# The start of a 12-stage network on one core: x loaded first, its squares summed along rows, scale before shift

## The chip, the cores and the metric

The kernel runs on one core of one Trainium2 chip. The metric is the device time of one execution in microseconds (us). Five engines work side by side, each with its own queue of instructions: TensorE (PE, matrix products), VectorE (DVE), ScalarE (ACT), GpSimd (POOL) and SyncE (SP, which here only starts transfers). They wait for each other through semaphores. An engine's transfers are carried by DMA queues: SP's go through q1, ACT's through q10, POOL's through q0, all on the same 16 DMA engines.

## The reference, cut to what matters

The network has twelve stages (a gated linear recurrence, sparse attention, differential attention, a state-space layer and feed-forward layers). The change lies wholly in what comes before the first matrix product of the first of them:

```python
c_act = jax.nn.silu(c)
mods = jnp.einsum('bd,lde->lbe', c_act, ada_w) + ada_b[:, None, :]
shift, scale, gate = jnp.split(mods[0], 3, axis=-1)

def rms_norm(x, gain):
    y = x32 * lax.rsqrt(jnp.mean(x32 * x32, axis=-1, keepdims=True) + EPS)
    return (y * gain).astype(x.dtype)

h = rms_norm(x, norm_mix[0]) * (1 + scale[:, None, :]) + shift[:, None, :]
q, f, i, g = jnp.split(h @ w_in, ...)          # the first matrix product
```

x is 512 tokens by 1024 features. c has 1024 entries, and the layer's shift and scale are 2 x 1024 numbers from a 1024 x 2048 piece of ada_w. All data are float32.

## The kernel before, in words

Features lie on the partitions: xT holds x as 8 tiles (kt = 0 to 7) of 128 features by 512 tokens. x arrives as rows (xin, 4 tiles of 128 tokens by 1024) and TensorE turns it, four 128x128 transposes a tile, into banks 0 to 3 of PSUM. ScalarE makes the square of each turned tile (sq, two buffers) and copies the tile to xT (lines 2160, 2161). TensorE multiplies sq by a matrix of ones, so that bank 7 holds the sum of squares of each token, on all partitions (line 535). ScalarE makes rstd = 1/sqrt(mean + eps) of it (2177, 2178).

The modulation: c and the biases come in as rows (vec_a), TensorE turns them, VectorE copies them to cols_a, and ScalarE makes cact = silu(c), 8 columns of 128. The 1024 x 2048 piece of ada_w arrives in 8 slices of 128 rows (ada_first, 1 MB each, 6 buffers; slices 6 and 7 wait on SP until slices 0 and 1 were used). Columns 0 to 1535 of each slice are taken by VectorE, which multiplies them by cact and adds them up in ada_sum (lines 524, 527); at the end TensorE sums ada_sum over the partitions with 12 products of one column (line 556). Columns 1536 to 2047 are taken by TensorE directly, 4 products of one column a slice (line 544). Each such product is two passes (float32) in the trace. All 16 results are columns of PSUM bank 4: 0 to 7 are shift, 8 to 15 are scale. VectorE adds the bias (mods, 2381), makes gain = (1 + scale) x norm_mix (gains_a, 2373), and signals mods_rdy.

A weight product is done in three parts for accuracy: weights as whi + wlo, activations as hh + hl. ScalarE rounds raw to whi (line 385), VectorE makes wlo = raw - whi (line 389). Then `apply` runs over the eight tiles: VectorE xn = xT x gain x rstd (2402), ScalarE hh = rounded xn + shift (2185), VectorE hl = xn + shift - hh (2394). TensorE's first block of products waits for wlo and takes each tile as hh and hl come (lines 426, 430); later blocks are line 448. raw has two buffers, and the load of the third block waits for wlo of the first.

The order on each engine is the order in which the code is written. On TensorE it is: turn vec_a; slices 0 and 1; x with its ones products; slices 2 to 7, with the transpose of vec_b (the norm gains, for cols_b) after slice 3; the 12 sums. The x load stands sixth in ScalarE's queue of issues, behind the constants; `ones` is the last of these, and TensorE's first instruction waits for all of them (const_a).

Of the kernel before, what the change touches and what calls it, by code (L numbers as in the profile page):

```python
# [17 lines left out]
ACT = mybir.ActivationFunctionType  # L18
# [51 lines left out]
def build(nc, a, out, upto=99):  # L70
    ctx = ExitStack()
    with ctx:
# [162 lines left out]
        const_a, const_in = sem("const_a_in"), sem("const_in")  # L235
        x_in = sem("x_in")
        sq_rdy, ssq_rdy, rstd_rdy = sem("sq_rdy"), sem("ssq_rdy"), sem("rstd_rdy")
# [280 lines left out]
        def ada_first_dve(dve, link):  # L518

            for kt in range(FIRST):  # L520
                dve.wait_ge(ada0_in[kt % 6], 16 * (kt // 6 + 1))
                w, c = ada_first[:, kt % 6, 0:NV * P], cact[:, kt:kt + 1]
                if kt == 0:
                    nc.vector.tensor_scalar(ada_sum[:, :], w, c, None, ALU.mult).then_inc(ada0_sum_v, 1)
                else:
                    dve.wait_ge(ada0_sum_v, kt)
                    nc.vector.scalar_tensor_tensor(out=ada_sum[:, :], in0=w, scalar=c, in1=ada_sum[:, :],
                                                   op0=ALU.mult, op1=ALU.add).then_inc(ada0_sum_v, 1)
            dve.wait_ge(cols_ps, 2)
            link(nc.vector.tensor_copy(cols_b[:, 0:NROW_B], ps[:, 5, 0:NROW_B]))  # L530

        def first_square_sum(pe, kt):

            pe.wait_ge(sq_rdy, kt + 1)
            nc.tensor.matmul(ps[:, 7, :], ones[:, :], sq[:, kt % 2, :], start=(kt == 0),
                             stop=(kt == KT - 1)).then_inc(ssq_rdy, 1)

        def ada_first_pe(pe, k0, k1):
# [15 lines left out]
            pe.wait_ge(ada0_sum_v, FIRST)  # L554
            for j in range(NV):
                m = nc.tensor.matmul(ps[:, 4, j:j + 1], ada_sum[:, j * P:j * P + P], ones[:, 0:1],
                                     start=False, stop=True, skip_group_check=True)
            m.then_inc(ada0_used, 1)

# [1494 lines left out]
        def _(sp):  # L2054

            for kt in range(FIRST):
                if kt >= 6:
                    sp.wait_ge(ada0_sum_v, kt - 5)
                    sp.wait_ge(ada0_used, kt - 5)
                sp.dma_start(ada_first[:, kt % 6, :], a["ada_w"][0, kt * P:(kt + 1) * P, 0:SLOT]  # L2060
                             ).then_inc(ada0_in[kt % 6], 16)
# [76 lines left out]
        def _(act):  # L2138
# [12 lines left out]
            act.dma_start(ones[:, :], a["k_ones"]).then_inc(const_a, 16)  # L2151
            act.dma_start(xin[:, :, :], a["x"][0].rearrange("(t p) d -> p t d", p=P)).then_inc(x_in, 16)
            act.wait_ge(cols_rdy, 1)
            nc.scalar.activation(cact[:, :], cols_a[:, ROWS["c"]:ROWS["c"] + 8], ACT.Silu).then_inc(cact_rdy, 1)
            log_table()
            for kt in range(KT):
                act.wait_ge(mm, kt + 1)
                if kt >= 2:
                    act.wait_ge(ssq_rdy, kt - 1)
                nc.scalar.activation(sq[:, kt % 2, :], ps[:, kt % 4, :], ACT.Square).then_inc(sq_rdy, 1)  # L2160
                nc.scalar.activation(xT[:, kt, :], ps[:, kt % 4, :], ACT.Copy).then_inc(ev_v, 1)
            act.wait_ge(pool_set, 2)

# [195 lines left out]
        def _(dve):  # L2359
# [20 lines left out]
            dve.wait_ge(cols_rdy, 1)  # L2380
            link(nc.vector.tensor_tensor(mods[:, 0:16], ps[:, 4, 0:16], cols_a[:, 0:16], ALU.add))
            modulated_gain(0, ROWS["norm_mix"], 8).then_inc(mods_rdy, 1)
            if upto >= 2:
                convert_lo(dve, segs[0], 0, 0, 0)

            def apply(j, m, gain, shift, h_free):
# [11 lines left out]
                for kt in range(KT):  # L2398
                    k = KT * j + kt
                    if k >= 2:  # L2400
                        dve.wait_ge(hl_rdy, k - 1)
                    nc.vector.scalar_tensor_tensor(out=xn[:, k % 2, :], in0=xT[:, kt, :],
                                                   scalar=gain[:, kt:kt + 1], in1=rstd[:, :],
                                                   op0=ALU.mult, op1=ALU.mult).then_inc(xn_rdy, 1)
                    if kt:
                        low(k - 1)
# [46 lines left out]
            if upto >= 2:  # L2453
                dve.wait_ge(mods_rdy, 1)
                apply(0, 0, *mod_cols(0), FIRST_UNITS)
# [124 lines left out]
        def _(pe):  # L2580
            pe.wait_ge(const_a, 16 * 5)
            nc.tensor.transpose(ps[:, 6, 0:NROW_A], vec_a[0:NROW_A, :], ident[0:NROW_A, 0:NROW_A]).then_inc(cols_ps, 1)
            ada_first_pe(pe, 0, 2)
            pe.wait_ge(x_in, 16)
            for kt in range(KT):
                if kt >= 4:
                    pe.wait_ge(ev_v, kt - 3)
                for t in range(TT):
                    m = nc.tensor.transpose(ps[:, kt % 4, t * P:(t + 1) * P], xin[:, t, kt * P:(kt + 1) * P],
                                            ident[:, :])  # L2590
                m.then_inc(mm, 1)
                if kt:
                    first_square_sum(pe, kt - 1)
            first_square_sum(pe, KT - 1)

# [55 lines left out]
            if upto >= 2:  # L2651
                ada_first_pe(pe, 2, FIRST)
                linear(seg["h_q"], need=(hl_rdy, 0))
# [131 lines left out]
```

## Time and profile before

| | |
|---|---|
| median of three runs | 3031.37 us (3028.98 to 3031.47) |
| the profiled execution | 3029.0 us, its span 3027.3 us |
| mean granted TensorE clock | 0.968 |
| busy share of the span | PE 93%, DVE 55%, ACT 35%, POOL 2% |
| start of the first weight product | 57.00 us |
| DMA | 321 MB, mean 106 GB/s; about 400 GB/s until 34 us, then none until 55 us |

Times in the views are us from the start of the span. Of a group "x16" the duration is from the first start to the last end. A float32 product shows as two passes, a transpose as one. The granted clock is given as a share of 2.4 GHz, so 0.50 is 1.2 GHz. PEld rows are weight loads, which overlap the products.

### The profile page before, as it was taken

The numbers are of one execution on the slowest core, as the hardware profiler recorded it, in microseconds if no ns is written. First come the engines' busy times: TensorE is split into PE (matmuls) and PEld (weight loads), VectorE is DVE, ScalarE is ACT, GpSimd is POOL, SyncE is SP. The second block draws the span as 40 slices with busy tenths as digits, with TensorE's granted clock in tenths as the row PEclk, the third lists the DMA queues.
The fourth block names the chain that finished last, engine by engine and source line by source line (L and its number), as shares of the span: only waits on it lengthen the run. The fifth ranks groups of instructions, "written<-read, shape, count | busy, mean of one in ns | idle before, by whom it ended". The sixth has DMA issues, their size and how long they took to land.

```text
span 3027.3 us, 38551 instructions
## 1 busy us (share of the span) xinstructions
PE 2827.0 (93%) x14850; PEld 2262.7 (75%) x14850; DVE 1654.6 (55%) x2383; ACT 1063.9 (35%) x1577; POOL 75.2 (2%) x87
## 2 busy tenths in 40 slices
PE   6999999999988799999999998999999977999999
PEld 4898778888776556688787785777887756778787
DVE  4576566766453667433334557467677395353342
ACT  3312233222322367332223438433232534342231
POOL 2013000000000000000000100000000000000000
PEclk9999999999999799999999999999999988999999
DMA  5640356564424000232333330143444671223332
GB/s 212 195 140 1 112 153 191 163 182 144 154 86 128 1 1 1 56 83 81 107 84 111 114 100 13 42 100 103 141 153 153 230 125 57 84 83 98 97 97 70
DMA packets 400811, 321.14 MB, mean 106 GB/s; under 512 B 14409, under 2 KB 387233, under 8 KB 399649
## 3 DMA queue, kind: packets, MB, share of 16 engines
q1 hardware_dynamic: 324096, 237.19, 26.7%
q10 hardware_dynamic: 74496, 77.77, 7.9%
q0 software_dynamic: 2080, 4.26, 0.6%
q8 instruction: 96, 1.57, 0.2%
q14 instruction: 43, 0.34, 0.0%
HBM read 293.05 MB, written 19.86 MB: 103 GB/s over the span
## 4 chain that ended last, share of the span: by engine, by line
PE 64%; issue 22%; DVE 8%; ACT 2%; DMA 2%; POOL 1%; SPq 0%; ACTq 0%; DVEq 0%; POOLq 0%
PE ps L448 45%; PE ps L426 4%; PE ps L442 2%; PE ps L430 2%; DVE ada_acc L1749 1%; PE ps L873 1%; PE ps L903 1%; PE ps L885 1%; PE ps L1617 1%; PE ps L2605 1%; DVE h_area L1751 1%; DVE h_area L1753 1%; DMA xin<-in_x 1%; PE ps L1658 1%; POOL kT L1829 1%
## 5 line engine op out<-in xcount | busy, mean ns | idle before, releaser
L448 PE MATMUL ps<-hh,whi 128*128 128x512 f32 x1744 | 690.8, 396 | 5.1 <-DVE xT L2439 1.6
L448 PE MATMUL ps<-hh,wlo 128*128 128x512 f32 x1744 | 680.7, 390 | 0.0
L448 PE MATMUL ps<-hl,whi 128*128 128x512 f32 x1744 | 680.1, 390 | 0.0
L389 DVE TENSOR_TENSOR wlo<-raw,whi 128x2048 fp32r<-128x2048 f32 x198 | 453.9, 2292 | 359.7 <-ACT whi L385 359.7
L385 ACT ACTIVATE whi<-raw 128x2048 fp32r<-128x2048 f32 x198 | 377.3, 1906 | 380.8 <-PE ps L448 257.7
L448 PEld LDWEIGHTS ps<-hh,whi 128*128 128x128 f32 x1744 | 328.1, 188 | 79.3 <-issue 11.8
L448 PEld LDWEIGHTS ps<-hl,whi 128*128 128x128 f32 x1744 | 328.2, 188 | 70.3 <-issue 3.8
L448 PEld LDWEIGHTS ps<-hh,wlo 128*128 128x128 f32 x1744 | 327.9, 188 | 69.2
L448 PE MATMUL ps<-hid_h,whi 128*128 128x512 f32 x756 | 307.4, 407 | 0.0
L448 PE MATMUL ps<-hid_l,whi 128*128 128x512 f32 x756 | 298.9, 395 | 0.0
L448 PE MATMUL ps<-hid_h,wlo 128*128 128x512 f32 x756 | 298.8, 395 | 0.0
L448 PEld LDWEIGHTS ps<-hid_h,whi 128*128 128x128 f32 x756 | 142.2, 188 | 37.5 <-issue 4.3
L448 PEld LDWEIGHTS ps<-hid_l,whi 128*128 128x128 f32 x756 | 142.2, 188 | 37.4 <-issue 4.3
L448 PEld LDWEIGHTS ps<-hid_h,wlo 128*128 128x128 f32 x756 | 142.0, 188 | 34.6
L510 DVE SCALAR_TENSOR_TENSOR ada_ring<-ada_ring,cact 128x256 f32<-128x256 f32 (+1 forms) x336 | 151.8, 452 | 12.1
L2202 ACT ACTIVATE sq<-xT 128x512 f32 (+1 forms) x56 | 35.3, 632 | 291.5 <-DVE xT L2439 138.8
L2437 DVE TENSOR_TENSOR xT<-xT,ps 128x512 f32 (+1 forms) x40 | 27.4, 686 | 165.8 <-PE ps L448 144.7
L2263 ACT ACTIVATE hid_h<-hid_f 128x512 f32 (+1 forms) x44 | 27.8, 632 | 246.6 <-DVE hid_f L2485 246.6
L426 PE MATMUL ps<-hh,whi 128*128 128x512 f32 x176 | 78.0, 443 | 38.4 <-ACT hh L2185 38.4
L2325 ACT ACTIVATE act_t<-ps 128x512 f32<-128x512 f32 x64 | 38.0, 597 | 194.8 <-PE ps L448 185.9
L2539 DVE TENSOR_TENSOR hid_f<-act_t 128x512 f32<-128x512 f32 x64 | 43.4, 688 | 103.7 <-ACT act_t L2325 103.3
L2485 DVE TENSOR_TENSOR hid_f<-act_t,ps 128x512 f32<-128x512 f32 x44 | 30.2, 687 | 126.3 <-PE ps L448 121.3
(401 smaller groups left out, 4130.8 us busy)
## 6 DMA issues: line engine op xcount, KB each, us to landing
raw<-in_ffn_w_in SPq DMA_DIRECT2D x44, 1024.0 KB, 6.0
ada_ring<-in_ada_w ACTq DMA_DIRECT2D x82, 512.0 KB, 4.4
raw<-in_ffn_w_up SPq DMA_DIRECT2D x32, 1024.0 KB, 5.4
raw<-in_ffn_w_down SPq DMA_DIRECT2D x32, 1024.0 KB, 5.8
raw<-in_ffn_w_out SPq DMA_DIRECT2D x32, 704.0 KB, 4.6
raw<-in_hgrn_w_in SPq DMA_DIRECT2D x16, 1024.0 KB, 5.8
raw<-in_attn_w_qkv SPq DMA_DIRECT2D x12, 1024.0 KB, 5.1
s_area<-cp_dram SPq DMA_DIRECT2D x6, 2048.0 KB, 9.8
```

Source lines behind the costliest of these rows:

```text
L385: nc.scalar.activation(whi[:, par, :], raw[:, par, :], ACT.Copy).then_inc(w_hi, 1)
L389: nc.vector.tensor_tensor(wlo[:, par, :], raw[:, par, :], whi[:, par, :].bitcast(F32), ALU.subtract).then_inc(w_lo, 1)
L426: nc.tensor.matmul(ps[:, 2 * par + j, :], tile(w, kt, j), hi[:, kt, :], start=(kt == 0 and n == 0), stop=False)
L430: m = nc.tensor.matmul(ps[:, 2 * par + j, :], tile(wh, kt, j), lo[:, kt, :], start=False, stop=(kt == k - 1))
L442: m = nc.tensor.matmul(ps[:, bank, half * 256:half * 256 + 256], x[:, kt, t0:t0 + P], w[:, kt, :], start=(kt == 0 and n == 0), stop=(kt == ...
L448: m = nc.tensor.matmul(ps[:, bank, :], tile(w, kt, j), x[:, kt, :], start=(kt == 0 and n == 0), stop=(kt == k - 1 and n == 2))
L510: nc.vector.scalar_tensor_tensor(out=acc if last else w[:, 0, :], in0=w[:, kt, :], scalar=cact[:, kt:kt + 1], in1=w[:, 0, :], op0=ALU.mult ...
L873: m = nc.tensor.matmul(ps[:, S_BANK[w % 2] + i, 0:n], nqr[rows, p, t * P:(t + 1) * P], (k_sel, k_win)[br][rows, p // 2, 0:n], start=False, ...
L885: m = nc.tensor.transpose(ps[:, 2 + i, kt * P:(kt + 1) * P], pbuf[:, 2 * (w % P_SLOTS) + i, kt * P:(kt + 1) * P], ident[:, :])
L2202: nc.scalar.activation(sq[:, q:q + 1, :], xT[:, bass.ds(b * s.dve + j, 1), :], ACT.Square).then_inc(sq_rdy, 1)
L2325: nc.scalar.activation(act_t[:, j, :], ps[:, 2 * par + j, :], ACT.Relu).then_inc(ev_a, 1)
L2539: nc.vector.tensor_tensor(hid_f[:, j, :], act_t[:, j, :], act_t[:, j, :], ALU.mult).then_inc(hidf_rdy, 1)
```

## The change

Four things are changed. x is loaded by SP ahead of all modulation weights, instead of by ScalarE behind the constants. The squares are no longer made from the turned tiles: ScalarE squares each 128-token row tile of xin whole (128x1024) with a running sum along the row, which gives four columns x_ssq of one sum a token. VectorE spreads each column onto the diagonal of a 128x128 tile (ident times the column, in the space of rstd, line 540 of the new kernel), and TensorE multiplies the four by ones (line 547), which puts the sums into bank 7 in the old layout. TensorE's order becomes: x first, with slice 0 after tile 3 and slice 1 after tile 7, then slices 2 and 3, the four ones products, and slices 4 to 7. And of the 12 final sums those of scale come first (four of them, bank 4) with their own signal, then the eight of shift into bank 6; VectorE makes scale, gain and the first two xn before it waits for shift.

```diff
+        def first_square_spread(dve):
+            for t in range(TT):
+                dve.wait_ge(x_sq, t + 1)
+                nc.vector.tensor_scalar(rstd[:, t * P:(t + 1) * P], ident[:, :], x_ssq[:, t:t + 1], None, ALU.mult
+                                        ).then_inc(sq_rdy, 2)
+        def first_square_sums(pe):
+            for t in range(TT):
+                pe.wait_ge(sq_rdy, 2 * t + 2)
+                nc.tensor.matmul(ps[:, 7, t * P:(t + 1) * P], ones[:, :], rstd[:, t * P:(t + 1) * P], start=True, stop=True,
+                                 skip_group_check=True).then_inc(ssq_rdy, 2)
...
-            for j in range(NV):
-                m = nc.tensor.matmul(ps[:, 4, j:j + 1], ada_sum[:, j * P:j * P + P], ones[:, 0:1],
-                                     start=False, stop=True, skip_group_check=True)
-            m.then_inc(ada0_used, 1)
+            for bank, part in ((4, range(KT, NV)), (6, range(KT))):
+                for j in part:
+                    m = nc.tensor.matmul(ps[:, bank, j:j + 1], ada_sum[:, j * P:j * P + P], ones[:, 0:1],
+                                         start=(j == 0), stop=True, skip_group_check=True)
+                m.then_inc(ada0_used, 1)
...
+            sp.dma_start(xin[:, :, :], a["x"][0].rearrange("(t p) d -> p t d", p=P)).then_inc(x_in, 16)
             for kt in range(FIRST):
...
-            act.dma_start(xin[:, :, :], a["x"][0].rearrange("(t p) d -> p t d", p=P)).then_inc(x_in, 16)
...
+            act.wait_ge(x_in, 16)
             for kt in range(KT):
                 act.wait_ge(mm, kt + 1)
-                if kt >= 2:
-                    act.wait_ge(ssq_rdy, kt - 1)
-                nc.scalar.activation(sq[:, kt % 2, :], ps[:, kt % 4, :], ACT.Square).then_inc(sq_rdy, 1)
                 nc.scalar.activation(xT[:, kt, :], ps[:, kt % 4, :], ACT.Copy).then_inc(ev_v, 1)
+                if kt % 2:
+                    t = kt // 2
+                    if t >= 2:
+                        act.wait_ge(x_sq, t - 1)
+                    nc.scalar.activation((sq, xn)[t % 2][:, :, :].rearrange("p s n -> p (s n)"), xin[:, t, :], ACT.Square,
+                                         accum_out=x_ssq[:, t:t + 1]).then_inc(x_sq, 1)
...
-            link(nc.vector.tensor_tensor(mods[:, 0:16], ps[:, 4, 0:16], cols_a[:, 0:16], ALU.add))
-            modulated_gain(0, ROWS["norm_mix"], 8).then_inc(mods_rdy, 1)
-            if upto >= 2:
+            link(nc.vector.tensor_tensor(mods[:, 8:16], ps[:, 4, 8:16], cols_a[:, 8:16], ALU.add))
+            link(modulated_gain(0, ROWS["norm_mix"], 8))
+            def first_shift():
+                dve.wait_ge(ada0_used, FIRST + 2)
+                nc.vector.tensor_tensor(mods[:, 0:8], ps[:, 6, 0:8], cols_a[:, 0:8], ALU.add).then_inc(mods_rdy, 1)
                 convert_lo(dve, segs[0], 0, 0, 0)
...
+                    if j == 0 and kt == 1:
+                        first_shift()
...
-            ada_first_pe(pe, 0, 2)
             pe.wait_ge(x_in, 16)
             for kt in range(KT):
...
-                if kt:
-                    first_square_sum(pe, kt - 1)
-            first_square_sum(pe, KT - 1)
+                if kt % 4 == 3:
+                    ada_first_pe(pe, kt // 4, kt // 4 + 1)
+            ada_first_pe(pe, 2, 4)
+            first_square_sums(pe)
...
-                ada_first_pe(pe, 2, FIRST)
+                ada_first_pe(pe, 4, FIRST)
```

TensorE at the start of the program, in the kernel before. `ada_first` with `cact` are the column products of a slice, `xin` the transposes, `sq` the squares' products; the semaphore waited for stands in brackets.

```order
1 L2582 MATMUL ps<-ident,vec_a 128x120 [waits const_a_in]
2 L544 MATMUL ps<-cact,ada_first 128x1 [waits ada0_in0,cact_rdy]
3 L544 MATMUL ps<-cact,ada_first 128x1 x3
4 L544 MATMUL ps<-cact,ada_first 128x1 [waits ada0_in1]
5 L544 MATMUL ps<-cact,ada_first 128x1 x3
6 L2589 MATMUL ps<-ident,xin 128x128 [waits x_in]
7 L2589 MATMUL ps<-ident,xin 128x128 x7
8 L535 MATMUL ps<-sq,ones 128x512 [waits sq_rdy]
9 L2589 MATMUL ps<-ident,xin 128x128 x4
10 L535 MATMUL ps<-sq,ones 128x512 [waits sq_rdy]
```

The same place in the changed kernel, down to the second slice (between the rows shown, four more groups of four transposes follow slice 0, each waiting for ev_v, a copy by ScalarE):

```order
1 L2603 MATMUL ps<-ident,vec_a 128x120 [waits const_a_in]
2 L2609 MATMUL ps<-ident,xin 128x128 [waits x_in]
3 L2609 MATMUL ps<-ident,xin 128x128 x15
4 L556 MATMUL ps<-cact,ada_first 128x1 [waits ada0_in0,cact_rdy]
5 L556 MATMUL ps<-cact,ada_first 128x1 x3
6 L2609 MATMUL ps<-ident,xin 128x128 [waits ev_v]
7 L2609 MATMUL ps<-ident,xin 128x128 x3
```

Sixteen transposes now stand ahead of slice 0, and slice 1 has moved behind all 32; after the transposes TensorE has this:

```order
14 L556 MATMUL ps<-cact,ada_first 128x1 [waits ada0_in1,cact_rdy]
16 L556 MATMUL ps<-cact,ada_first 128x1 [waits ada0_in2,cact_rdy]
18 L556 MATMUL ps<-cact,ada_first 128x1 [waits ada0_in3]
20 L562 MATMUL ps<-ident,vec_b 128x120 [waits const_in]
21 L547 MATMUL ps<-rstd,ones 128x128 [waits sq_rdy] x4
22 L556 MATMUL ps<-cact,ada_first 128x1 [waits ada0_in4,cact_rdy]
24 L556 MATMUL ps<-cact,ada_first 128x1 [waits ada0_in5]
```

The eight 512-wide products of the squares have become four 128-wide ones between slices 3 and 4. (Of each slice the first product is shown; three more follow it.)

VectorE around the modulation, in the kernel before:

```order
9 L527 SCALAR_TENSOR_TENSOR ada_sum<-ada_first,cact,ada_sum 128x1536 [waits ada0_sum_v,ada0_in1]
10 L530 COPY cols_b<-ps 128x120 [waits cols_ps]
11 L2381 TENSOR_TENSOR mods<-ps,cols_a 128x16 [waits cols_rdy,ada0_used,v_link]
12 L2373 SCALAR_TENSOR_TENSOR gains_a<-mods,cols_b 128x8 [waits v_link]
13 L389 TENSOR_TENSOR wlo<-raw,whi 128x2048 [waits w_hi]
14 L2402 SCALAR_TENSOR_TENSOR xn<-xT,gains_a,rstd 128x512 [waits mm,rstd_rdy,mods_rdy]
15 L2402 SCALAR_TENSOR_TENSOR xn<-xT,gains_a,rstd 128x512
16 L2394 SCALAR_TENSOR_TENSOR hl<-xn,mods,hh 128x512 [waits hh_rdy]
```

And in the changed kernel:

```order
5 L527 SCALAR_TENSOR_TENSOR ada_sum<-ada_first,cact,ada_sum 128x1536 [waits ada0_sum_v,ada0_in3]
6 L540 TENSOR_SCALAR rstd<-ident,gains_a 128x128 [waits x_squares] x4
7 L527 SCALAR_TENSOR_TENSOR ada_sum<-ada_first,cact,ada_sum 128x1536 [waits ada0_sum_v,ada0_in4]
12 L2398 TENSOR_TENSOR mods<-ps,cols_a 128x8 [waits cols_rdy,ada0_used,v_link]
13 L2390 SCALAR_TENSOR_TENSOR gains_a<-mods,cols_b 128x8 [waits v_link]
14 L2422 SCALAR_TENSOR_TENSOR xn<-xT,gains_a,rstd 128x512 [waits mm,rstd_rdy,v_link]
15 L2422 SCALAR_TENSOR_TENSOR xn<-xT,gains_a,rstd 128x512
16 L2403 TENSOR_TENSOR mods<-ps,cols_a 128x8 [waits ada0_used]
17 L389 TENSOR_TENSOR wlo<-raw,whi 128x2048 [waits w_hi]
18 L2414 SCALAR_TENSOR_TENSOR hl<-xn,mods,hh 128x512 [waits hh_rdy]
```

The spreads stand between slices 3 and 4 and wait there for the squares; gain and two xn stand ahead of the second wait for TensorE, and wlo behind it.

## Rows read from the trace of the kernel before

**Rows 1.** The page: the chain that ended last, by line.

```profile
PE ps L448 45%; PE ps L426 4%; PE ps L442 2%; PE ps L430 2%; DVE ada_acc L1749 1%; PE ps L873 1%; PE ps L903 1%; PE ps L885 1%; PE ps L1617 1%; PE ps L2605 1%; DVE h_area L1751 1%; DVE h_area L1753 1%; DMA xin<-in_x 1%; PE ps L1658 1%; POOL kT L1829 1%
```

**Rows 2.** The chain of waits, 0 to 75 us: start, duration, what.

```profile
3.54 25.71 DMA xin<-in_x
...
29.29 1.97 PE ps L2589 x8
...
43.99 3.59 PE ps L544 x32
47.59 5.13 PE ps L556 x24
...
53.09 2.28 DVE wlo L389
...
70.63 4.37 PE ps L448 x18
```

**Rows 3.** The timeline, 14 to 70 us: start, duration, instruction, idle time before.

```profile
14.92 0.46 PE L2582 MATMUL ps<-ident,vec_a 120*128 120x120 f32 x1 [14.92 <-DMA ones<-in_k_ones]
...
15.96 1.28 ACT L642 ACT_TABLE_LOAD   x1
...
16.00 3.57 PE L544 MATMUL ps<-cact,ada_first 128*128 128x1 f32 x16 [0.62 <-ACT cact L2154]
...
29.71 1.82 DVE L527 SCALAR_TENSOR_TENSOR ada_sum<-ada_first,cact,ada_sum 128x1536 f32<-128x1536 f32 x1 [1.18 <-DMA ada_first<-in_ada_w]
...
56.89 0.75 DVE L2394 SCALAR_TENSOR_TENSOR hl<-xn,mods,hh 128x512 fp32r<-128x512 f32 x1 [0.19 <-ACT hh L2185]
...
57.00 0.77 PE L426 MATMUL ps<-hh,whi 128*128 128x512 f32 x1 [4.29 <-ACT hh L2185]
...
69.76 1.09 ACT L2222 ACTIVATE qT<-ps 128x512 f32<-128x512 f32 x2 [0.21 <-PE ps L430]
```

**Rows 4.** Stretches: busy time and count of each engine, clock, DMA.

```profile
47.00:53.00 6.00, 5.71 (x29) 5.62 (x28) 0.17 (x1) 0.00 (x0) 0.00 (x0) 0.52 0.00 0
...
57.00:60.40 3.40, 3.40 (x8) 2.75 (x9) 3.33 (x5) 1.68 (x3) 3.20 (x6) 0.50 0.91 284
60.40:66.00 5.60, 5.60 (x25) 4.58 (x25) 5.46 (x9) 2.69 (x5) 4.41 (x7) 0.96 0.00 1
...
2372.00:2375.00 3.00, 3.00 (x15) 2.50 (x16) 3.00 (x5) 1.02 (x1) 0.00 (x0) 0.50 0.57 162
2375.00:2378.00 3.00, 3.00 (x29) 3.00 (x28) 1.49 (x3) 2.55 (x3) 0.00 (x0) 0.98 1.11 328
```

**Rows 5.** DMA queues: packets, MB; q10 to 3 us, both 3-14, both 14-28.

```profile
q10 hardware_dynamic: 16, 0.00, 0.8%
...
q1 hardware_dynamic: 574, 4.19, 93.1%
q10 hardware_dynamic: 429, 0.19, 6.2%
...
q1 hardware_dynamic: 504, 3.73, 64.5%
q10 hardware_dynamic: 519, 2.09, 36.7%
```

**Rows 6.** DMA issues: third slice (1.7 us), first weight block (20.0), to landing.

```profile
L2060 SPq DMA_DIRECT2D ada_first<-in_ada_w x1: 427/427/427, 1.7 to 1.7; - x1
DMA to landing us min/median/max: 10.0/10.0/10.0
...
raw<-in_hgrn_w_in SPq DMA_DIRECT2D x1, 1024.0 KB, 12.7
```

**Rows 7.** Groups by form, whole span (last row: to 80 us): busy us, mean ns.

```profile
L981 ACT ACTIVATION_READ_ACCUMULATOR nsa_area<-ps,nsa_area 128x1 f32 x128 | 25.6, 200 | 0.0
...
L973 ACT ACTIVATE nsa_area<-ps 128x1024 f32<-128x1024 f32 x16 | 16.4, 1026 | 0.0
...
L506 DVE TENSOR_SCALAR ada_ring<-ada_ring,cact 128x256 f32<-128x256 f32 x1 | 0.4, 354 | 0.9 <-DMA ada_ring<-in_ada_w 0.9
```

More of the change, by code:

```diff
@@ L235, in build @@
         const_a, const_in = sem("const_a_in"), sem("const_in")
-        x_in = sem("x_in")
+        x_in, x_sq = sem("x_in"), sem("x_squares")
         sq_rdy, ssq_rdy, rstd_rdy = sem("sq_rdy"), sem("ssq_rdy"), sem("rstd_rdy")
@@ L528, in ada_first_dve @@
                                                    op0=ALU.mult, op1=ALU.add).then_inc(ada0_sum_v, 1)
+                if kt == 3:
+                    first_square_spread(dve)
             dve.wait_ge(cols_ps, 2)
             link(nc.vector.tensor_copy(cols_b[:, 0:NROW_B], ps[:, 5, 0:NROW_B]))
[L532 to L536, printed above, removed]
+        x_ssq = gains_a[:, 4, 0:TT]
+        def first_square_spread(dve):
[8 more added lines that the diff above has]
+                                 skip_group_check=True).then_inc(ssq_rdy, 2)
         def ada_first_pe(pe, k0, k1):
@@ L2453, in _ @@
             if upto >= 2:
-                dve.wait_ge(mods_rdy, 1)
                 apply(0, 0, *mod_cols(0), FIRST_UNITS)
@@ L2588, in _ @@
                 for t in range(TT):
-                    m = nc.tensor.transpose(ps[:, kt % 4, t * P:(t + 1) * P], xin[:, t, kt * P:(kt + 1) * P],
-                                            ident[:, :])
+                    m = nc.tensor.transpose(ps[:, kt % 4, t * P:(t + 1) * P],
+                                            xin[:, t, kt * P:(kt + 1) * P], ident[:, :])
                 m.then_inc(mm, 1)
-                if kt:
-                    first_square_sum(pe, kt - 1)
-            first_square_sum(pe, KT - 1)
+                if kt % 4 == 3:
+                    ada_first_pe(pe, kt // 4, kt // 4 + 1)
+            ada_first_pe(pe, 2, 4)
+            first_square_sums(pe)
             def square_sums(s, m, b, par):
```

## The prediction

> **What bounds the kernel now.** The page of the profile comes first: TensorE is busy 93% of the span, and 45% of the chain that ended last are its weight products of line 448 alone [rows 1]. The change touches none of them. It touches what runs before the first one, so the view that counts is the chain of waits over the first 75 us, and it holds hardly any slack [rows 2]. The chain is: x lands at 29.25, TensorE turns it and sums its squares until 42.1, then finishes the column products with the modulation weights (slices 2 to 7, the last four of them in 3.59 us) and the final sums (5.13 us), until 52.7. VectorE makes wlo of the first block until 55.4, two normalised tiles follow, and the first weight product starts at 57.00, with the first low half hl at 56.89 [rows 3]. From there on VectorE's pairs of xn and hl and then TensorE carry the time. Nothing later is tied to an absolute moment: the next weights are asked for when wlo is done. So what the prologue loses or wins in front of hl moves the rest with it.
>
> Two things of the prologue are not visible in the chain. VectorE's sum over the modulation weights ended at 29.71 + 1.82 = 31.5 and lay idle until TensorE came to it 16 us later [rows 3]. And TensorE's clock: 16 passes of one column took 3.57 us at 16.0, and at 43.99 twice as many took 3.59 [rows 2, 3]. The first are at the lower level (1.2 GHz), which the record of the granted clock does not show that early. From 47 to 53 it reads 0.52 [rows 4], and 24 passes take 5.13, 0.44 us for a product of two passes against 0.23 before it fell. The fall came after 5 us in which one-column products were all TensorE had.
>
> **The transfers.** Two hardware queues take turns packet by packet: from 14 to 28 us q1 moved 504 packets of 8 KB and q10 519 of 4 KB, which is x [rows 5]. So x, last in q10 behind small constants, landed only with the tenth MB. Now x stands first in SP's queue. The rate hardly depends on the mixture (4.38 MB in 11 us, 5.82 MB in 14 us: 398 and 416 GB/s [rows 5]), the bytes and their order behind x are the same, so position decides: the third MB landed at 1.7 + 10.0 = 11.7 [rows 6]. With x as the first two MB, x lands near 9 and slice 0 of the modulation weights near 11.7, each further slice 2.56 us later (1.05 MB at 410), and slice 7 at 29.7, exactly as now, since both orders put ten MB ahead of that moment. The first hgrn block still lands at 20.0 + 12.7 = 32.7 [rows 6]; its whi takes 1.9 and is ready at 34.6.
>
> The small constants release everything: ones landed at 14.92 [rows 3]. Their 24 packets per engine each waited behind an 8 KB packet (574 in 11 us on 16 engines, 0.31 us each [rows 5]). Those that meet x's 4 KB packets wait half. If all meet them, ones lands 24 x 0.155 = 3.7 us earlier, at 11.2; if none, at 14.9. Up to 3 us q10 had moved 16 of its packets, though its first issue stands at 0.82 like that of SP [rows 5]; so part of x will be gone before they meet it, and I take the value nearer to none: 1.5 us, ones at 13.4.
>
> **x and its squares.** Before, each of eight tiles cost a Square and a Copy on ScalarE and a 512-wide ones product on TensorE, 12.8 us from 29.29 to 42.1. Now there are 8 copies at a pitch of 0.5 us (two such evacuations in 1.09 [rows 3]) and 4 squares of 128x1024 with a sum. No such square is in the trace; the nearest rows are 1.03 us for 128x1024 and 0.20 for reading an accumulator [rows 7], so 1.2 each (0.8 if the read is hidden, 1.5 if the sum slows the pass; the four together move by 1.6 at most). The column chain from ones to the loaded table took 15.96 + 1.28 - 14.92 = 2.3 us [rows 3], so ScalarE starts at 15.7 and ends at 15.7 + 8 x 0.5 + 4 x 1.2 = 24.5. TensorE's first 16 transposes (0.25 each at the low clock, eight in 1.97 [rows 2]) end at 17.8, the column products of slice 0 at 19.6, the remaining transposes, paced by ScalarE, at 22.8. rstd follows the ones products (below, 26.8) and is ready by 28.2, before anybody needs it.
>
> SP's wait moves as well: slice 6 is asked for when TensorE has used slice 0 (19.6, now 18.0), slice 7 after slice 1 (24 to 25, now 19.6). The queue still holds 9 MB until 25.5, so this costs nothing unless ones is late; then up to 2 us.
>
> **VectorE.** Slices 0 to 3 are done by 21.3, as they land. Then the four diagonal spreads, 128x128 each, bounded by the 0.35 of the 128x256 row [rows 7] and taken at 0.2, stand in front of slice 4 and wait for the last square, 24.5. Behind them are queued slices 4 to 7: 24.9 + 4 x 1.82 = 32.2. This added wait makes VectorE 0.7 us later than the 31.5 of now.
>
> **TensorE up to the shift.** After 22.8 it has 12 products (slices 1 to 3), the vec_b transpose, four 128x128 ones products, 16 products (slices 4 to 7), then 4 for scale and 8 for shift. The clock decides. I take the first 12 at 0.23 (to 25.6), 1.2 us for the next two items (26.8), and the clock fallen by then, because again only one-column products ran for some 5 us: 16 x 0.44 = 7.0 to 33.8. That is past VectorE's 32.2, so TensorE is what is late next. Scale 4 x 0.44 gives 35.6, shift 8 x 0.44 gives 39.1. Behind scale VectorE makes the gain and two xn tiles (0.35 + 1.4 us, done by 37.4), work that the 3.5 us of shift hides; before, it stood in the path. ScalarE waits with hh and GpSimd with its memset for the shift; both are ready sooner than today. After the shift: 0.3 us, wlo 2.28, hl at 41.7. Before it was 56.89. The sum is 15.2 us, and the first products start at 41.75 for 57.00, again at the low clock as in the trace [rows 4], so that stretch is merely displaced.
>
> Does the clock rise at all now? The 512-wide sums are gone, only transposes are left. At 2372.0 TensorE ran 15 transposes in 3.00 us at a granted 0.50 and then 29 in 3.00 us at 0.98, and nothing else [rows 4]. So transposes alone raised it. The Trainium skill, "TensorE: Matmul & The Clock Gate" (Part 4: PE-mode transpose), says that the full clock does not engage for transposes, as they do not count as busy. This trace disagrees for its 64-column ones; by the page the case is the second rival.
>
> **Rivals.**
> Full clock to the end: the transposes and bursts keep 2.4 GHz. Then VectorE's 32.2 is the bound, 12 x 0.235 gives 35.0, plus 2.6 is 37.6: gain 19.3, profiled 3009.7. Against it: the fall at 47 under denser one-column work than this. Chance 0.20.
> Low clock throughout: 32 transposes and slice 0 take 9.7 from 13.9 (23.6), 12 x 0.446 = 5.4, 1.5 for the two items, 16 x 0.446 = 7.1 (37.6), 5.3 for the sums, plus 2.6 is 45.5: gain 11.4, profiled 3017.6. For it: ScalarE's pacing leaves the transposes with gaps, which those at 2372 did not have. Chance 0.25.
> ones lands at 14.9 all the same: everything above 1.5 later, gain 13.7, 3015.3. Chance 0.06.
> The gain does not arrive (a later stage takes it back): no absolute time in the code speaks for it; 3029. Chance 0.02.
> Slower: the clock after the first products. Now it rises at about 60.4, 3.4 us after they start [rows 4], and stays. If the changed lead-in left it at 1.2 GHz in the first dense blocks, each 10 us of products would cost 10 more, and beyond 15 us of them the gain is gone; over the four blocks of h_q, some 40 us of products (192 at 0.23; 18 took 4.37 [rows 2]), the result is 26 slower, 3055. Against it: dense products raised it at 60.4, and transposes at 2375 [rows 4]. Chance 0.02.
> My forecast has the remaining 0.45.
>
> **The numbers.** The profiled execution took 3029.0 (span 3027.3 and 1.7 around it); 3029.0 - 15.2 = 3013.8. The three runs lie from 3028.98 to 3031.47, median 3031.37; from their middle, 3030.2, it is 3015. The range takes in both clock rivals on either baseline: 3028.98 - 19.3 = 3009.7 and 3031.47 - 11.4 = 3020.1, so 3010 to 3020. A difference under 0.2% (6 us) can't be told from none. Every case but two gains over 11: faster 0.96, same 0.02, slower 0.02.
>
> **What would show it.** x landing near 9 and slice 7 still near 29.7; ones between 11 and 15; the last square near 24.5; VectorE's sum ended near 32; the 16 products in front of scale at 0.44 each, ending after it; first hl near 41.7. I am wrong if one-column products run at 0.23 to the end, if slice 7 lands later than 30.5 (SP's wait), or if the distance from first hl to the end of the span changes by more than 2 us.

## The result, and the profile after

The changed kernel takes 3016.83 us (median of 5 runs, 3015.55 to 3018.63); the kernel before, run beside it, 3031.47 (5 runs, 3028.98 to 3037.92). The ratio is 0.995, with a 95% interval from 0.9935 to 0.9964: 14.6 us faster, half a percent. The prediction was 3015, with a range from 3010 to 3020. The profiled executions are closer together, 3029.0 and 3017.62, which is 11.4 us; where the other 4 to 5 us of the pair went has a part of its own below.

The page first. The shares hardly move, as they must when 15 us of 3000 are at stake:

```profile
PE 2831.3 (94%) x14842; PEld 2270.5 (75%) x14842; DVE 1657.0 (55%) x2388; ACT 1064.9 (35%) x1577; POOL 76.4 (3%) x87
...
PE ps L448 45%; PE ps L426 4%; PE ps L442 2%; PE ps L430 2%; DVE ada_acc L1762 1%; PE ps L886 1%; PE ps L916 1%; PE ps L898 1%; PE ps L1630 1%; PE ps L2626 1%; DVE h_area L1764 1%; DVE h_area L1766 1%; PE ps L1671 1%; POOL kT L1842 1%; DMA ada_ring<-in_kv_ada_w 1%
```

In the chain by line [rows 1] the load of xin is gone from its 1%, and a load of ada_ring has the last place. All else stands there with lines moved by 13 to 21. The view that answers to [rows 2] is the chain of waits over the first 43 us (start, duration, what):

```profile
3.06 10.75 DMA ones<-in_k_ones
...
13.86 0.46 PE ps L2603
14.32 3.41 PE ps L2609 x16
17.73 1.50 PE ps L556 x8
19.23 3.38 PE ps L2609 x16
22.61 2.57 PE ps L556 x24
25.18 0.16 PE ps L562
25.35 1.24 PE ps L547 x8
26.58 6.62 PE ps L556 x32
33.20 5.13 PE ps L569 x24
...
38.36 0.17 DVE mods L2403
38.52 2.21 DVE wlo L389
...
40.78 2.07 PE ps L426 x4
```

The chain no longer waits for x: the constants release TensorE at 13.86, and from there to 38.3 it never pauses. L2609 are the transposes, L556 the column products of the slices, L547 the squares' products, L569 the final sums. The same 16 transposes per half take 3.4 us at either place (0.21 each), the 12 products of slices 1 to 3, two passes each, run at 0.21 a product, and the 16 of slices 4 to 7 at 0.41. The first weight product starts at 40.78 for 57.00 [rows 3].

The timeline of the same stretch shows the parts beside the chain; it answers to [rows 3]:

```profile
23.56 1.06 ACT L2177 ACTIVATE xn<-xin 128x1024 f32<-128x1024 f32 x1
...
24.51 0.21 ACT L2177 ACTIVATION_READ_ACCUMULATOR xn<-xin 128x1 f32 x1
...
24.82 0.29 DVE L540 TENSOR_SCALAR rstd<-ident,gains_a 128x128 f32<-128x128 f32 x1 [1.72 <-ACT xn L2177]
...
25.02 7.58 DVE L527 SCALAR_TENSOR_TENSOR ada_sum<-ada_first,cact,ada_sum 128x1536 f32<-128x1536 f32 x4
...
34.08 1.91 ACT L385 ACTIVATE whi<-raw 128x2048 fp32r<-128x2048 f32 x1 [6.05 <-DMA raw<-in_hgrn_w_in]
...
40.64 0.74 DVE L2414 SCALAR_TENSOR_TENSOR hl<-xn,mods,hh 128x512 fp32r<-128x512 f32 x1
```

The spread is named rstd<-ident,gains_a because x_ssq is a piece of gains_a. The last square with its read ends at 24.72, VectorE waits 1.72 for it and then sums the last four slices to 32.60. That is ahead of TensorE, which reaches the final sums at 33.20. The clock, in the columns of [rows 4]:

```profile
22.60:26.50 3.90, 3.90 (x36) 3.90 (x34) 1.97 (x3) 2.12 (x6) 0.00 (x0) 0.90 1.01 422
26.50:33.00 6.50, 6.50 (x33) 6.50 (x32) 5.99 (x5) 1.32 (x2) 0.00 (x0) 0.50 1.04 373
33.00:38.30 5.30, 5.30 (x25) 5.23 (x25) 1.75 (x4) 1.91 (x1) 0.00 (x0) 0.50 0.43 136
40.80:46.00 5.20, 5.20 (x12) 4.10 (x13) 5.06 (x8) 2.17 (x3) 5.03 (x6) 0.50 0.71 202
46.00:50.00 4.00, 4.00 (x18) 3.26 (x17) 3.93 (x6) 2.00 (x3) 3.79 (x7) 0.97 0.00 0
```

By the durations the clock rose at about 22.3, behind the transposes (0.21 us each up to there, a pass of a slice 0.107 us behind it); the granted clock reads 1.00 from the start on and doesn't show this rise. The clock fell again between 25 and 26.5, behind the 12 one-column products of slices 1 to 3 (2.57 us), the transpose of vec_b and the squares' products, and rose again at about 46, 5 us after the first weight products (3.4 us in the kernel before [rows 4]).

### The profile page after: what moved, and what is told of

It reads as the page before. It is cut to its first block, busy times and chain, and to the rows that moved or that the text cites. A ratio compares the mean times of both kernels' runs of the same rounds, so it can differ in the third digit from the quotient of the medians.

```text
span 3015.9 us, 38545 instructions
## 1 busy us (share of the span) xinstructions
PE 2831.3 (94%) x14842; PEld 2270.5 (75%) x14842; DVE 1657.0 (55%) x2388; ACT 1064.9 (35%) x1577; POOL 76.4 (3%) x87
## 4 chain that ended last, share of the span: by engine, by line
PE 65%; issue 22%; DVE 8%; ACT 2%; DMA 2%; POOL 1%; SPq 0%; ACTq 0%; DVEq 0%; POOLq 0%
PE ps L448 45%; PE ps L426 4%; PE ps L442 2%; PE ps L430 2%; DVE ada_acc L1762 1%; PE ps L886 1%; PE ps L916 1%; PE ps L898 1%; PE ps L1630 1%; PE ps L2626 1%; DVE h_area L1764 1%; DVE h_area L1766 1%; PE ps L1671 1%; POOL kT L1842 1%; DMA ada_ring<-in_kv_ada_w 1%
## 5 line engine op out<-in xcount | busy, mean ns | idle before, releaser
L426 PE MATMUL ps<-hh,whi 128*128 128x512 f32 x176 | 78.4, 445 | 36.5 <-ACT hh L2202 34.1
```

What stands on the lines that cost most here:

```text
L426: nc.tensor.matmul(ps[:, 2 * par + j, :], tile(w, kt, j), hi[:, kt, :], start=(kt == 0 and n == 0), stop=False)
```

## The experiments

Each row is one profile. "hl" is the start of the first low half, up to which the prologue counts; "rest" is the span less that start. All times are us; ratios are to the kernel before, beside it on the same chip. The kernels ran on several chips, so ratios can be compared between rows and medians can't.

| kernel | hl | rest | time, median | ratio and interval |
|---|---|---|---|---|
| before, as shown | 56.89 | 2970.4 | 3031.47 | 1 |
| before, again | 59.99 | 2975.2 | 3036.92 (one run) | |
| changed, as shown | 40.64 | 2975.3 | 3016.83 | 0.9950 (0.9935 to 0.9964) |
| changed, second | 40.65 | 2973.0 | 3014.58 | 0.9942 (0.9929 to 0.9955) |
| changed, third | 40.68 | 2972.6 | 3014.99 (one run) | |
| x load alone | 45.60 | 2970.5 | 3023.04 | 0.9972 (0.9963 to 0.9982) |
| split of the sums alone | 58.23 | 2970.8 | 3030.73 | 0.9987 (0.9977 to 0.9997) |
| changed without the split | 42.24 | 2979.0 | 3016.31 | 0.9949 (0.9936 to 0.9962) |
| changed, squares by tile | 43.38 | 2972.9 | 3021.49 | 0.9967 (0.9955 to 0.9979) |
| wide products late | 44.52 | 2974.2 | 3021.06 | 0.9954 (0.9941 to 0.9968) |
| wide products early | 46.66 | 2976.9 | 3021.81 | 0.9953 (0.9940 to 0.9967) |
| constants first | 43.83 | 2973.7 | 3018.62 | 0.9946 (0.9932 to 0.9961) |
| both of these | 46.28 | 2972.6 | 3020.29 | 0.9950 (0.9937 to 0.9963) |
| ones by memset | 40.39 | 2976.1 | 3017.34 | 0.9939 (0.9925 to 0.9952) |

**The x load alone.** The kernel before with one line moved:

```diff
         def _(sp):
+            sp.dma_start(xin[:, :, :], a["x"][0].rearrange("(t p) d -> p t d", p=P)).then_inc(x_in, 16)
             for kt in range(FIRST):
...
-            act.dma_start(xin[:, :, :], a["x"][0].rearrange("(t p) d -> p t d", p=P)).then_inc(x_in, 16)
```

> The kernel before with one edit: SP loads x ahead of the modulation weights. Theory 'the load was the bound': TensorE no longer waits for x but goes on right behind slices 0 and 1, which it finishes at about 18.5 instead of waiting until 29.25, so all behind it comes 10.7 us earlier: first hl at 46 to 46.5 against 56.89, some two thirds of the 16.25 us. Rival 'the new squares and order bring it': less than 6 us, hl later than 51.

Its hl stands at 45.60, 11.3 earlier than before and a little earlier than the 46 to 46.5 expected, and the rival (later than 51) is out; the timed ratio, 0.9972, is 8.5 us. Of the change's 16.25 at hl, and of the 17.6 us timed beside this kernel (0.9942), that is two thirds and one half. So the order of the loads alone is the largest part. Its chain:

```profile
32.78 3.51 PE ps L544 x32
```

The 512-wide products of the squares (L535) come between the transposes here, and the clock is up until the last slices are done: their 32 passes cost 3.51, where the changed kernel pays 6.62. In this pair of profiles the gain of the change's other parts is paid in part with that. But the squares' products don't ensure it: with the same products in place, these 32 passes took 3.59 and 6.16 in the two profiles of the kernel before.

**The split alone, and the change without it.** The edit of the second takes back the pieces on the final sums and on `first_shift`; the first adds them to the kernel before:

```diff
-            for j in range(NV):
...
+            for bank, part in ((4, range(KT, NV)), (6, range(KT))):
```

> The kernel before with one edit: the four sums of scale first, then the eight of shift with their own signal, gain and two xn made between. Theory: the shift's eight sums (3.5 us) hide the gain and two xn (1.6 us), so the first hl comes 1.5 us earlier than 56.89, at 55.3 to 55.5. Rival (nothing gained, because ScalarE's hh or wlo is late anyway): hl within 0.3 of 56.89.

> The changed kernel without the scale-before-shift part: all twelve final sums into one bank with one signal, wlo before the first two xn, as before. Theory: two xn tiles (1.42 us) and the gain (0.2) come back onto the path behind the last sum, so the first hl is 1.5 us later than 40.64, at 42.1 to 42.3, and the time is longer by 1.5. Rival (the split only moves the wait of VectorE, since TensorE's sums end at the same time): hl within 0.3 of 40.64.

The two stand for one another only when the clock is taken out. On the changed kernel the split is worth 42.24 - 40.64 = 1.6, as expected. The two profiles took another course up to the sums, though: without the split they started at 32.8 for 33.1, held by slice 7 (below), and from there to hl it is 9.5 for 7.6, so that the split itself makes 1.9. On the kernel before hl comes 1.3 later, not earlier, which neither theory had; the chain says why:

```profile
44.93 5.87 PE ps L544 x32
50.80 5.13 PE ps L557 x24
```

From the sums to hl the split saves what it should, 58.23 - 50.80 = 7.43 for 56.89 - 47.59 = 9.30 [rows 2, 3], which is 1.9. But slices 4 to 7 took 5.87 for 3.59 [rows 2], because the clock had fallen sooner, and the part with x began slower. The second profile of the unchanged kernel shows that this is no doing of the split:

```profile
44.53 6.16 PE ps L544 x32
```

Same program, 6.16 for 3.59. The timed runs of the split alone, 0.9987 with an interval up to 0.9997, agree with a gain of one to two us and can't tell it from much less; those of the changed kernel with and without it (0.9942 and 0.9949) can't be told apart.

**The squares by tile, in the changed order.** ScalarE squares each turned tile and TensorE sums it in 512-wide products, as before, x staying first:

```diff
-            act.wait_ge(x_in, 16)
...
+                nc.scalar.activation(sq[:, kt % 2, :], ps[:, kt % 4, :], ACT.Square).then_inc(sq_rdy, 1)
...
+                if kt:
+                    first_square_sum(pe, kt - 1)
...
-            first_square_sums(pe)
```

> The changed kernel with the squares in the old form: ScalarE squares each turned tile and TensorE sums with a 512-wide ones product, x still first. Theory 'TensorE and ScalarE carry the x part': it takes its 12.8 us again instead of 8.5, slice 1 is used at about 29 instead of 23, so slice 7 is issued and lands 5 us later (35 to 36), and the first hl comes at 44 to 46, 4 to 5 us later than 40.64. Rival 'clock': the dense 512-wide products keep TensorE at its upper level, the column products behind them run at 0.23 us, and most of the loss is won back: hl at 41 to 43.

hl comes at 43.38, 2.7 later than with row squares: earlier than the 44 to 46 of the first theory and just past the 41 to 43 of the rival. The timed runs agree (0.9967 against 0.9942, the two intervals meeting at 0.9955). In the chain:

```profile
31.05 4.89 PE ps L560 x32
```

The slices after the x part begin at 31.05 for 26.58, and the clock, up until then, gives a part back: 4.89 for 6.62. So the row squares win less than the 4.5 us of work they take out.

**Can the clock be kept up?** Two kernels put wide products with no use between the slices, whose result nobody reads: three 512-wide ones behind slices 5 to 7, or seven 256-wide ones behind slices 1 to 7.

```diff
+                if kt >= 5:
+                    pe.wait_ge(ev_v, KT)
+                    nc.tensor.matmul(ps[:, 0, :], ones[:, :], xT[:, 0, :], start=True, stop=True)
```

> The changed kernel plus three products of 512 columns without a use (ones by a tile of xT, into a bank that is overwritten later), one behind each of the slices 5, 6 and 7 on TensorE. Theory 'clock': they fill the time in which TensorE would wait for slices and keep it at the upper level, so the twelve sums take 2.6 to 2.9 us instead of 5.26; shift is then ready at 35.5, the first weights (landed 34.1, rounded 36.0) are what is late next, and hl is at 38.2 to 38.5 instead of 40.64. Rival 'work': the clock falls all the same, the three products cost 0.86 to 1.7 us each on a TensorE that has no room: hl at 42 to 45.

> The changed kernel plus a product of 256 columns without a use behind each of the slices 1 to 7 on TensorE, so that 512-column work (two passes of 256 each) stands between the one-column products from 22 us on, before the clock fell at 25 to 26. Theory 'one-column products alone let it fall, wide ones between them hold it': the clock stays at 1.00 until the first weight product; the sums take 2.6 to 2.9 us and hl is at 38.2 to 39.2. Rival 'half the time is not enough': it falls at 25 to 29 all the same, the seven products cost 0.43 each at the high and 0.86 at the low level on a TensorE that is late already, and hl is at 43 to 46.

Neither did, and in both the rival's case came. The first, from 25 to 37 us:

```profile
25.00:37.00 12.00, 12.00 (x40) 8.98 (x40) 7.01 (x5) 3.23 (x3) 0.00 (x0) 0.50 0.88 316
```

The clock had fallen before the first of them and stayed at 0.50 over all three (1.92 us each in the chain), and hl is 3.9 later. The second kernel began earlier, at 23.8, when the clock was up:

```profile
22.50:26.50 4.00, 4.00 (x31) 3.90 (x30) 1.94 (x3) 2.24 (x6) 0.00 (x0) 1.00 1.02 426
26.50:39.00 12.50, 12.50 (x51) 11.64 (x51) 6.01 (x5) 3.23 (x3) 0.00 (x0) 0.50 0.72 250
```

It fell at 26.5 all the same, in the third wide product (0.54, 0.54 and 0.80 us); the rest cost 1.06 each, and hl is 6.0 later. So wide products in these two forms are no remedy. The last slice runs at the lower clock in each order tried without the squares' own products, and with them in three of five profiles at least in part (slices 4 to 7 in 3.51 and 3.59, but 4.89, 5.87 and 6.16). The final sums take 4.9 to 5.3 us, the lower level, in every kernel.

**The constants first.** SP waits for the constants between x and the slices; a further kernel has this and the late wide products:

```diff
             sp.dma_start(xin[:, :, :], a["x"][0].rearrange("(t p) d -> p t d", p=P)).then_inc(x_in, 16)
+            sp.wait_ge(const_a, 16 * 5)
```

> The changed kernel with one wait on SP: x is issued first, and the slices of the modulation weights only once the five constants have landed. Theory 'the slices hold the constants back': their packets began only at 5 us although they were issued from 0.8 us on, because TensorE's constants share the way with five or six larger loads issued at the same time; alone beside x they land by 7 to 8, no bubble arises (x keeps the engines busy until 7), TensorE starts when x lands (9.6) instead of at 13.9, and slice 7 (29.7) is late next: hl at 39.0 to 39.6. Rival 'bubble': the constants need x's end in any case and the slices start late by 1 to 3 us, which shifts slice 7 and the first weights by as much: hl at 41 to 44.

> Both: the wait on SP and the three 512-wide products. If both theories hold, the first weights (landed, rounded at 36.0) bound it: hl at 38.2 to 38.5, and no better than the products alone. If the gate costs a bubble of 1 to 3 us in the transfers, hl at 39.5 to 41.5. If the clock falls all the same: 41 to 45.

The constants landed and TensorE started 3.4 us earlier, at 10.47, and hl came 3.2 later, at 43.83: the rival 'bubble'. The chain of the first, and its stretch from 8 to 11 us:

```profile
10.45 5.03 DMA ada_first<-in_ada_w
...
21.17 13.16 DMA ada_first<-in_ada_w
...
34.38 1.87 PE ps L556 x8
```

```profile
8.00:11.00 3.00, 0.53 (x3) 0.53 (x4) 0.03 (x1) 0.00 (x0) 1.87 (x4) 1.00 0.29 70
```

Between x's last packet and the first slice's SP's queue lies idle: 70 GB/s for 387 in the changed kernel. From the issue of a slice to its landing there pass 5.0 us even with an empty queue, and every later slice carries the hole: slice 7 lands at 34.3. The kernel with both edits has hl at 46.28, past everything that was expected of it; its loss of 5.6 is less than the two losses together (3.2 and 3.9). The timed ratios of these four kernels (0.9946 to 0.9954) don't confirm their losses of 3 to 6 us at hl, and don't exclude them: their intervals overlap the changed kernel's.

**Ones without a load.** What releases TensorE at 13.86 is the last constant. GpSimd can write it:

```diff
+            nc.gpsimd.memset(ones[:, :], 1.0).then_inc(ones_set, 1)
...
-            act.dma_start(ones[:, :], a["k_ones"]).then_inc(const_a, 16)
...
-            pe.wait_ge(const_a, 16 * 5)
+            pe.wait_ge(const_a, 16 * 4)
+            pe.wait_ge(ones_set, 1)
```

> The changed kernel with the matrix of ones written by GpSimd instead of loaded. It takes 128 of the 376 small packets out of ScalarE's queue, a third of the rounds in which they take turns with the packets of x and the slices. Theory 'TensorE is one unbroken chain from the constants on': TensorE starts 2 to 2.6 us earlier, at 11.2 to 11.9; the chain then meets slice 7, which still lands near 30.1 and takes 1.8 us on either engine, so the final sums start at 31.9 to 32.2 instead of 33.1, and the first hl comes at 39.5 to 39.9 instead of 40.64. Rival 'slices bound it already': sums and hl within 0.3 of the old times. Rival 'clock': TensorE's stretches of high and low clock fall otherwise and move hl by 1 us or more either way.

```profile
10.42 0.46 PE ps L2604
...
20.39 10.50 DMA ada_first<-in_ada_w
...
30.93 1.87 PE ps L556 x8
```

TensorE starts 3.44 earlier, more than expected, and hl moves only from 40.64 to 40.39, which is what the rival 'slices bound it already' allows (0.3). The last slice of the modulation weights is now what is late: it lands at 30.9, and TensorE's and VectorE's shares of it end at 32.8 and 32.7. So bounds that nearly tie hold the sums at 33: TensorE's work from 13.9, VectorE's (to 32.6 in the changed kernel), and slice 7. The time, 0.9939 with an interval from 0.9925, can't be told from the changed kernel's; no kernel tried is clearly better than that.

**The same kernels again.** Unchanged copies, to see what repeats: the changed kernel twice, the kernel before once.

> The changed kernel once more, for a second profile. Both theories: the first hl again at 40.6 us within 0.5, since the prologue is one unbroken chain. They differ behind it. In the first pair of profiles the stretch from the first hl to the end of the span grew by 4.9 us (2970.4 to 2975.3). Theory 'chance' (the low-clock stretches of TensorE fall elsewhere in each execution): this time the stretch differs from 2975.3 by 1 us or more in either direction. Rival 'system' (the changed start takes it back every time): 2975.3 within 0.7. Time 3014 to 3018.

> The changed kernel once more, for a third profile. First hl at 40.6 within 0.5. The stretch behind it was 2975.3 and 2973.0. Theory 'chance': anything from 2970 to 2979, with the steps against the kernel before at other places than in the first two. Rival 'system': never below 2972.5.

> The kernel before once more, for a second profile. First hl at 56.9 within 1.5 (the clock's fall during the column products decides). Theory 'chance': the stretch from the first hl to the end of the span, 2970.4 in the first profile, comes out between 2970 and 2979 as in the changed kernels. Rival 'system': the old prologue has the short stretch every time, 2970.4 within 0.5 (as the two kernels with one edit each, 2970.5 and 2970.8), and the new prologue costs 2 us or more behind hl.

The changed kernel's hl is 40.64, 40.65 and 40.68, though its clock takes another course in the third profile. There the clock rose at about 16, within the first 16 transposes, the x part ended 3 us earlier, and slice 7 held the end:

```profile
13.93 2.92 PE ps L2609 x16
16.85 0.79 PE ps L556 x8
17.64 1.98 PE ps L2609 x16
...
20.48 10.71 DMA ada_first<-in_ada_w
...
31.23 1.87 PE ps L556 x8
```

The kernel before has no such second bound: its hl is 56.89 and 59.99, with the clock, where 1.5 of difference was expected at most. And the rest behind hl differs between profiles of one and the same kernel by 4.8 (before) and 2.7 (changed). Of the two theories 'system' is out: the kernel before isn't held to 2970.4, and the changed kernel's second profile is 2.3 from its first. The third alone (2972.6) fits both.

## Why the prediction was right, and where it was not

**The transfers.** x landed 8.8 after its issue at 0.82, at 9.6 (near 9 was said), slice 7 at 30.1 (29.7). ones landed at 13.86: of the 3.7 us that x's smaller packets could have given it got 1.1, near the 1.5 taken (13.6 and 13.5 in the second and third profile, against the forecast's 13.4); the rival of 14.9 is out. The first hgrn block came at 34.1, not 32.7, for SP asked for it at 23.85 and no longer at 20.0. The prediction said that the later wait of SP costs nothing, and named slices 6 and 7 alone; this block it left out. It cost nothing all the same, since whi was ready at 36.0 and the shift only at 38.3. How close slice 7 is to the path was missed. In the second and third profile of the changed kernel it landed at 31.2, asked for at 23.3 and at 20.5, against 30.1 in the first, asked for at 23.5. That is past the 30.5 that the prediction named as a sign of being wrong, and not by SP's wait, which it gave as the reason: the one asked for 3 us sooner came no sooner. What holds it up, no run shows. In the second profile VectorE waits for it:

```profile
31.18 1.82 DVE L527 SCALAR_TENSOR_TENSOR ada_sum<-ada_first,cact,ada_sum 128x1536 f32<-128x1536 f32 x1 [0.72 <-DMA ada_first<-in_ada_w]
```

VectorE ends at 33.0 there and TensorE's sums start at 33.05. So "TensorE is what is late next" is true of the first profile by 0.6 us (33.2 against VectorE's 32.6), where the prediction had 1.6; the second is a tie, and in the third slice 7 is late.

**The squares.** 1.06 and 0.20 for a square and its read, 1.2 taken; the last ended at 24.7 (24.5). The spreads took 0.29, not 0.2, and VectorE ended at 32.6 (32.2), still before TensorE.

**TensorE and the clock.** This was the term that decided between the rivals, and in the first two profiles its course was the forecast's: up with the transposes, down at slices 4 to 7. The prediction gave as its reason 5 us of one-column products alone; its own sum has only 2.8 us of them and 1.2 us of other work there, so the time of the fall was partly luck. Their cost was 6.62 (7.0), slices 1 to 3 took 2.57 (2.8), the sums began at 33.1 (33.8), shift ended at 38.3 (39.1), hl came at 40.64 (41.7). Of the 1.1 us, 0.6 lies in the two stretches of column products, which the prediction had at 0.44 and 0.23 each and the trace has at 0.41 and 0.21; the rest is spread over the final sums and wlo. The rivals of full clock to the end (37.6) and of low clock throughout (45.5) are both out in all three profiles, though in the third slice 7 and not the clock sets the same hl. Like the transposes of [rows 4], the 32 of 128x128, with one slice's products between them, brought the clock up, at about 22.3, and in the third profile the first 16 alone did (0.12 us each behind it for 0.21). The Trainium skill, "TensorE: Matmul & The Clock Gate" (Part 4: PE-mode transpose), would have it stay down; the trace disagrees.

**The parts, as measured.** Of the 16.25 us by which hl comes earlier, the x load makes 56.89 - 45.60 = 11.3, the row squares with TensorE's new order 45.60 - 42.24 = 3.4, and the split 42.24 - 40.64 = 1.6. These are single profiles. The first part compares two profiles in which slices 4 to 7 ran at the upper clock (3.59 and 3.51 us), the second one of these with a kernel that has the lower clock at the end. The two profiles of the kernel before differ by 3.1 at hl, and the x load alone may differ as much, as its slices may meet the lower clock too. So the first part can be anything from 8.6 (an estimate, 45.60 + 6.16 - 3.51 = 48.25 against 56.89) to 14.4 (59.99 - 45.60), and only the changed kernel's own hl is known to repeat (to 0.04).

**What was luck.** The 15.2 us were taken from the one profile of the kernel before that had hl at 56.89. Taken from the other, 59.99, the same sum gives 18.3, and the measured gain at hl is 16.25 or 19.35. That the time came within 2 us of 3015 rests in part on this: the first hl was 1.1 earlier than forecast, and the stretch behind it 4.9 longer than assumed.

**The step that failed: that the prologue's gain moves the rest with it unchanged, with less than 2 us of difference behind hl.** The rest was 2970.4 before and 2975.3 after, 4.9 more. The profiled pair therefore shows 11.4 of the 16.25. One stage carries as much as all of it: three groups of the state-space stage, in the kernel before

```profile
2372.00 8.65 PE L1592 MATMUL ps<-ident,h_area 128*64 128x128 f32 x64 [3.75 <-DVE h_area L1737]
2381.98 4.20 PE L1600 MATMUL ps<-ident,s_area 64*128 64x64 f32 x64 [1.33 <-ACT s_area L1680]
2386.89 28.80 PE L1617 MATMUL ps<-s_area 128*128 128x128 f32 x256 [0.71 <-ACT s_area L1686]
```

in the changed kernel

```profile
2354.87 9.88 PE L1605 MATMUL ps<-ident,h_area 128*64 128x128 f32 x64 [3.75 <-DVE h_area L1750]
2366.00 6.19 PE L1613 MATMUL ps<-ident,s_area 64*128 64x64 f32 x64 [1.25 <-ACT s_area L1693]
2372.88 31.01 PE L1630 MATMUL ps<-s_area 128*128 128x128 f32 x256 [0.69 <-ACT s_area L1699]
```

and in its second profile

```profile
2369.55 4.19 PE L1613 MATMUL ps<-ident,s_area 64*128 64x64 f32 x64 [1.29 <-ACT s_area L1693]
```

The sums are 41.65 and 47.08, 5.4 apart; the other differences behind hl cancel to half a microsecond. In the changed kernel's second profile the middle group is back at 4.19. The granted clock goes with it: from 2367 to 2376 it reads 0.52 in the changed kernel, where the middle group runs, and from 2376 to 2386 it reads 1.00 in the kernel before, where its middle group runs.

```profile
2367.00:2376.00 9.00, 8.31 (x66) 8.12 (x65) 0.00 (x0) 4.49 (x8) 0.00 (x0) 0.52 0.61 215
```

```profile
2376.00:2386.00 10.00, 8.67 (x107) 8.43 (x105) 0.49 (x1) 9.12 (x14) 0.31 (x1) 1.00 1.03 389
```

This stage is not wholly chance. The three groups take 41.65 and 41.53 in the two profiles of the kernel before, and 47.08, 42.66 and 44.13 in those of the changed one, whose first group is always 1.0 us or more longer. With the late wide products, which leave the whole change in place, they take 41.64. The stage doesn't decide the rest, though: the kernel before had 41.53 here and a rest of 2975.2. The rest behind hl is 2970.4 and 2975.2 for the kernel before, 2975.3, 2973.0 and 2972.6 for the changed one: each spreads more than their means (2972.8 and 2973.6) differ. The kernels with wide products late have 2974.2 and 2972.6. In place of "under 2 us" the runs show that one profile of this kernel holds the rest to about 5. The two timings of the change, 14.6 and 17.6 us, lie on both sides of the prologue's 16.25. Whether a microsecond of the rest is systematic they can't tell, and that stays open.

## What to carry to other kernels

Look first at the order in which the first ten megabytes are asked for: one load moved from behind the weights to ahead of them made half to two thirds of this gain, and a gate meant to help the small loads through cost more at hl than it gave, because it emptied the queue. Price narrow TensorE products at both clock levels, whatever stands before them: the same 32 passes took 3.59 and 6.16 us in two profiles of one kernel. And a difference of a few microseconds between two profiles of a 3 ms kernel says nothing until a second profile of each is beside them; the distance from a common instruction shows which part repeats.

## What the runs showed of the hardware that was not expected

The small constants hardly move before about 5 us, in the changed kernel as well, though issued from 0.8 to 3: up to 3 us q10 has moved 16 packets, as before [rows 5]. The queues' rows from 3 to 5 us, where there is no q10, and from 5 to 8:

```profile
q1 hardware_dynamic: 166, 0.68, 93.4%
```

```profile
q10 hardware_dynamic: 180, 0.08, 9.6%
```

With the constants first it was the same (16 packets up to 3 us, none from 3 to 5, 193 from 5 to 8), so it is not the slices' issues that hold them. They ended sooner (10.47), when only x's packets stood between them.

Three 512-wide products in fp32 between one-column ones did not raise a fallen clock (0.50) in 12 us; each took 1.92 us. The weight products of the changed kernel saw it rise 5.2 us after their start, and its transposes did in all three profiles.
